# A decoder layer on one core: key products on VectorE in batches, rows turned for the expert gathers, and a new order of the attention steps

## The reference

```python
# sample: every token keeps 256 of 2049 keys, by indexer score, and attends to the gathered rows
_, idx = lax.top_k(sc, topk)
kg, vg = ck[phys, off], cv[phys, off]          # 256 rows of 512 floats per sample, keys and values
s = einsum('bthd,btkhd->bthk', q, kg) * 64**-0.5;  p = softmax(s);  out = einsum('bthk,btkhd->bthd', p, vg)
# prompt: 8 heads of sparse attention over <= 256 keys, mask from the indexer's top 64;
#         4 heads of attention into 256 memory tokens without a mask
m = g0 * (conv @ w_br_conv) + g1 * (attn @ w_br_attn) + g2 * (mem @ w_br_mem)
h = LN(ALPHA * x + m @ w_o)
# 32 experts (1024 -> 2*256 -> 1024), 2 per token inside the best of 4 groups
y = sum_e gate[:, e] * ((silu(h @ up_e[:, :256]) * (h @ up_e[:, 256:])) @ w_down[e])
out = LN(ALPHA * h + y)
```

## Time and profile before

| | |
|---|---|
| median of 3 runs | 612.38 us (610.49 to 614.92) |
| profiled execution, device time | 612.95 us |
| profiled execution, span of the records | 611.1 us, so 1.85 us lie around it |
| TensorE busy | 551.1 us (90%) |
| VectorE busy | 277.9 us (45%) |
| ScalarE busy | 101.1 us (17%) |
| GpSimd busy | 63.9 us (10%) |
| moved by DMA | 163.53 MB, 268 GB/s over the span |

### The profile page before, as it was taken

One profiled execution on the slowest core, in us unless ns is written; L12 is line 12 of the kernel. 1 busy time (PEld: TensorE's weight loads), 2 busy tenths in 40 slices (PEclk: granted clock), 3 DMA queues, 4 the chain that ended last, 5 costly groups with the idle time before them and its releaser, 6 DMA issues.

```text
span 611.1 us, 8674 instructions
## 1 busy us (share of the span) xinstructions
PE 551.1 (90%) x3518; PEld 348.4 (57%) x3518; DVE 277.9 (45%) x766; ACT 101.1 (17%) x243; POOL 63.9 (10%) x70
## 2 busy tenths in 40 slices
PE   7999999999999995999799899999999995987671
PEld 4556566475688773777576456766654661522120
DVE  1273765666677687759862496312010200100026
ACT  1001111011310123545100211011101110101011
POOL 0000000000200034587200000000000000000002
PEclk9999999998999996999899997999999999897796
DMA  8981231944443445576869926899999999999971
GB/s 294 372 321 45 93 138 50 365 140 140 131 132 120 139 138 189 175 242 190 330 247 403 321 70 262 306 417 388 424 390 422 420 419 420 422 419 421 417 302 71
DMA packets 47886, 163.53 MB, mean 268 GB/s; under 512 B 5954, under 2 KB 22812, under 8 KB 35812
## 3 DMA queue, kind: packets, MB, share of 16 engines
q1 hardware_dynamic: 39280, 139.81, 59.4%
q0 software_dynamic: 3472, 14.31, 6.9%
q10 hardware_dynamic: 5092, 8.83, 4.0%
HBM read 160.14 MB, written 2.77 MB: 267 GB/s over the span
## 4 chain that ended last, share of the span: by engine, by line
PE 57%; DMA 17%; DVE 17%; ACTq 5%; issue 2%; ACT 1%; SPq 0%; POOLq 0%; POOL 0%; DVEq 0%
PE bank L578 11%; DMA ring<-in_w_down 10%; PE bank L769 10%; PE bank L1122 6%; DMA ring<-in_w_up 5%; PE bank L539 4%; PE bank L1214 2%; PE bank L965 2%; ACTq L1476 2%; PE bank L624 2%; ACTq L1475 2%; DVE ring L1686 2%; PE bank L1079 2%; PE bank L1097 2%; PE bank L592 2%
## 5 line engine op out<-in xcount | busy, mean ns | idle before, releaser
L769 PE MATMUL bank<-work,ring 128*128 128x264 f32 x384 | 94.1, 396 | 0.0
L578 PE MATMUL bank<-ring,work 128*128 128x512 f32 (+2 forms) x224 | 90.6, 544 | 2.1 <-DMA ring<-in_w_in 2.1
L769 PEld LDWEIGHTS bank<-work,ring 128*128 128x128 f32 x384 | 71.2, 192 | 14.8 <-issue 2.8
L1122 PE MATMUL bank<-ring,work 128*32 128x512 f32 x304 | 52.4, 665 | 14.2 <-DMA ring<-in_w_up 11.0
L578 PEld LDWEIGHTS bank<-ring,work 128*128 128x128 f32 x224 | 40.0, 190 | 32.8 <-issue 29.7
L2350 DVE SCALAR_TENSOR_TENSOR work<-work,bank 128x256 f32<-128x256 f32 x8 | 3.4, 422 | 87.0 <-ACT work L1530 87.0
L2362 DVE COPY gates<-bank 128x512 f32<-128x512 f32 x8 | 5.5, 692 | 74.7 <-PE bank L1214 67.7
L895 PE MATMUL bank<-work,ring 128*128 128x264 f32 x128 | 32.6, 400 | 4.3 <-DVE gates L2091 4.3
L1122 PEld LDWEIGHTS bank<-ring,work 128*32 128x32 f32 x304 | 13.9, 121 | 37.5 <-issue 37.4
L1122 PE MATMUL bank<-proj,work 128*32 128x512 f32 x128 | 30.6, 622 | 2.3 <-DMA ring<-in_w_up 1.9
L895 PEld LDWEIGHTS bank<-work,ring 128*128 128x128 f32 x128 | 24.0, 195 | 12.5 <-DVE gates L2091 5.1
(11 more groups left out here) (337 smaller groups left out, 845.1 us busy)
## 6 DMA issues: line engine op xcount, KB each, us to landing
ring<-in_w_up SPq DMA_DIRECT2D x19, 2048.0 KB, 19.8
ring<-in_w_down SPq DMA_DIRECT2D x13, 2048.0 KB, 24.3
ring<-in_w_in SPq DMA_DIRECT2D x22, 1024.0 KB, 5.9
proj<-in_w_up SPq DMA_DIRECT2D x8, 2048.0 KB, 20.7
misc<-in_w_up SPq DMA_DIRECT2D x5, 1024.0 KB, 25.9
gates<-in_w_up SPq DMA_DIRECT2D x5, 1024.0 KB, 20.2
ring<-in_w_o SPq DMA_DIRECT2D x4, 1024.0 KB, 8.7
proj<-in_w_down SPq DMA_DIRECT2D x2, 2048.0 KB, 24.3
```

What stands on the lines that cost most here:

```text
L578: last = mm(bank[2 * (i % 2) + t][:, 0:w], lhs[:, k, 128 * t:128 * t + 128], rhs[:, k % 4, :], start=(k == 0), stop=(k == KT - 1))
L769: last = mm(b[:, 0:TOK], w[:, k, 128 * (n % 2):128 * (n % 2) + 128], xT[:, k, 0:TOK], start=(k == 0), stop=(k == KT - 1))
L1122: last = mm(bank[5][32 * j:32 * j + 32, :], xTe[q // 2 % 2][:, k, s0:s0 + CAP], up_of(n + j // 2, j % 2, r), start=(k == 0), stop=(k == KT ...
```

## The change

It has several parts, and none alters what is computed.

- **Keys.** GpSimd only issues DMAs: 16 key gathers without a wait between them, then 16 value gathers. VectorE multiplies all 17 key rows, in place and several rows to an instruction (groups 3, 4, 5, 2, 2 and 1 rows), and sums them likewise.
- **Memory heads.** `softmax(n)` for n < 4 no longer writes scaled scores: the maximum is taken from the score bank, two numbers are scaled, and `exps(n)` reads the bank with a scale of 0.125. `head_out(p)` moves to ScalarE.
- **Order in attention.** `scores(0)` moves ahead of `gate_tile(11)`, `softmax(0)`, `softmax(1)` and their inverses come earlier, no top-k round stands between index steps any more, `scores(p + 1)` stands between the two `turn`s of a pair, and three small VectorE steps move ahead of the compaction.
- **Order in the merge.** The last key products stand behind `merge(2)`; `sample_max` comes after `branch_tile(5)`, the later sample steps are put between other branch tiles.
- **Turned rows.** `h3` is stored turned, number k * 128 + q instead of q * 8 + k, so that a gather's weight operand is a run of 128 numbers. ScalarE copies tiles 0 and 2 from `ytmp` (`h_copied`), VectorE writes tile 1 (`ln_scale_turned`) and a second time untouched into `ytmp`. The ALPHA residual now reads `ytmp`: `residual_tile(0)` and `residual_samples` move in between parts of `wo_second`, `residual_tile(1)` behind `up_half(0, 1)`.
- **DMA.** The constant table waits for the first weight unit instead of `x`; a half of an expert's down weights (`down_0[1]`) is issued two positions later.

```diff
-KEY_PRODUCTS = ((), range(0, 3), range(3, 6), range(6, 9), range(9, 12), ())
-KEY_DOTS = ((), (), range(12, 13), range(13, 15), range(15, 17), ())
+KEY_SUMS = ((), ((0, 3),), ((3, 7),), ((7, 12),), ((12, 14),), ((14, 16), (16, 17)))
+        hturn = gate_t[:, 0:3072].rearrange("p (t k q) -> p t q k", t=3, k=KT)
...
@@ sync
                 if n == NU_WO:
-                    sp.wait_ge(kd_mul, NPROD)
-                    sp.wait_ge(kd_dot, NDOT)
+                    sp.wait_ge(kd_sum, NSUMS)
...
-                if p == NWS:
+                if p == NWS + 2:
                     sp.wait_ge(route_ready, 1)
                     sp.dma_start(down_0[1], e0[:, 1]).then_inc(aside_in, 16)
@@ tensor
             gate_tile(10)
             index_scores(0)
+            scores(0)
             gate_tile(11)
...
             index_scores(2)
-            scores(0)
             gate_tile(13, part=0)
...
                 turn(2 * p)
-                turn(2 * p + 1)
                 if p + 1 < PAIRS_H:
                     scores(p + 1)
-                ahead, behind = PAIR_TILES[p]
                 if p == 0:
                     gate_tile(14, part=1)
+                turn(2 * p + 1)
...
-                    sample_max(1, H)
                     branch_tile(4)
-                    branch_tile(5)
-                    sample_spread(1, H)
                 values(p)
...
+            branch_tile(5)
+            sample_max(1, H)
             branch_tile(6)
+            sample_spread(1, H)
             branch_tile(7)
+            branch_tile(8)
             sample_sum(1, H)
-            branch_tile(8)
             branch_tile(9)
...
-            wo_second(0, (0, 1, 2, 3, 4, 5, 7, 6)).then_inc(wo_ps, 1)
+            wo_second(0, (0, 1, 2, 3, 4))
+            pe.wait_ge(h_ready, 1)
+            pe.wait_ge(aid_ready, 1)
+            residual_tile(0).then_inc(res_ps, 1)
+            wo_second(0, (5, 7, 6)).then_inc(wo_ps, 1)
...
             wo_second(1, range(4))
+            pe.wait_ge(h_ready, 2)
+            residual_samples().then_inc(res_ps, 1)
...
-                        last = mm(bank[6 + b][:, 128 * kk:128 * kk + 128], h3[:, t, 4 * b + kk::KT], Ssl[:, t, 0:128],
+                        last = mm(bank[6 + b][:, 128 * kk:128 * kk + 128], h3[:, t, 128 * (4 * b + kk):128 * (4 * b + kk) + 128], Ssl[:, t, 0:128],
...
+            pe.wait_ge(h_ready, 3)
+            residual_tile(1)
             gate_turn(0)
@@ scalar
-            act.wait_ge(x2_in, 16)
-            act.dma_start(cst[:, 128:nconst], a["consts"][:, 128:nconst]).then_inc(cst_in, 16)
...
+            act.wait_ge(unit_sem(0), UC[0])
+            act.dma_start(cst[:, 128:nconst], a["consts"][:, 128:nconst]).then_inc(cst_in, 16)
...
+                    src, scale = (score_bank(n)[:, at:at + w], 0.125) if n < NMH else (s, 1.0)
+                    act.activation(s, src, ACT.Exp, bias=stats[:, st + t:st + t + 1], scale=scale,
...
+            def h_copied(n, t, m):
+                act.wait_ge(h_ready, n)
+                act.activation(hturn[0:m, t], ytmp[0:m, :].rearrange("p (q k) -> p q k", k=KT), ACT.Copy).then_inc(hp_ready, 1)
@@ gpsimd
-                pool.tensor_tensor(prod[i % 4], Kg[:, i, :], qrep, ALU.mult).then_inc(kd_mul, 1)
...
+            for i in range(16):
+                key_gather(i)
+            pool.wait_ge(sa_p, 4)
+            for i in range(16):
+                value_gather(i)
@@ vector
+            def key_sum(i0, i1):
+                if i0 == 0:
+                    dve.wait_ge(qr_sb, 1)
                     dve.wait_ge(knew_in, 32)
+                    dve.wait_ge(kg_in, 16 * 16)
+                n = i1 - i0
+                rows = Kg[:, i0:i1, :] if i0 < 16 else knew.unsqueeze(1)
+                tt(rows, rows, qrep.unsqueeze(1).broadcast_to([128, n, AW]), ALU.mult)
+                link(V.tensor_reduce(ssc[:, H * i0:H * i1].rearrange("p (i h) -> p i h", i=n),
+                                     rows.rearrange("p i (h d) -> p i h d", d=HD), AX.X, ALU.add), kd_sum)
...
+                if n < NMH:
+                    link(V.tensor_reduce(st[:, 0:2], score_bank(n)[:, :].rearrange("p (t n) -> p t n", t=2),
+                                         AX.X, ALU.max, negate=True))
+                    ts(st[:, 0:2], st[:, 0:2], 0.125, s=at_m)
+                    return
...
+            def ln_scale_turned(x, t, lnb, done_sem):
+                link(V.scalar_tensor_tensor(hturn[:, t], x.rearrange("p (q k) -> p q k", k=KT),
...
+            merge(2)
+            for i0, i1 in KEY_SUMS[PAIRS_H - 1]:
+                key_sum(i0, i1)
+            merge(3)
             sample_max(H, 17, sbias)
```

More of the change, by code:

```diff
@@ L978, in logits, with residual_tile, residual_samples @@
                 return last
+            def residual_tile(t):
+                for dh in range(2):
+                    last = mm(bank[2 * t + dh][:, :], alpha_id, ytmp[:, 512 * dh:512 * dh + 512], start=True, stop=False)
+                return last
+            def residual_samples():
+                for j in range(4):
+                    last = mm(bank[4][32 * j:32 * j + 32, 0:256], alpha_id[0:NS, 0:32],
+                              ytmp[0:NS, 256 * j:256 * j + 256], start=True, stop=False)
+                return last
             pe.wait_ge(r_ready, 1)
@@ L1035, in _ @@
             mm(bank[5][:, 64:96], ones[:, 0:128], mask[:, 0:32], start=False, stop=False)
-            mm(bank[5][:, 64:96], ones[:, 0:128], mask[:, 64:96], start=False, stop=True).then_inc(pos_ps, 1)
-            first_part(1, range(4), (0, 2))
+            mm(bank[5][:, 64:96], ones[:, 0:128], mask[:, 64:96], start=False, stop=True)
+            for t in range(3):
+                last = mm(bank[5][:, 96:128], ones[:, 0:128], mask[:, 32 * t:32 * t + 32], start=(t == 0), stop=(t == 2))
+            last.then_inc(pos_ps, 1)
+            pe.wait_ge(hp_ready, 3)
             pe.wait_ge(first_s, 2)
-            pe.wait_ge(h_ready, 3)
             for b in range(2):
                 first_part(b, range(4), (1,)).then_inc(first_ps, 1)
-            for t in range(3):
-                last = mm(bank[3][:, 0:32], ones[:, 0:128], mask[:, 32 * t:32 * t + 32], start=(t == 0), stop=(t == 2))
-            last.then_inc(cnt2_ps, 1)
+            pe.wait_ge(cnt_read, 1)
             def first_gather(i):
@@ L1464, in _ @@
                     normalise(2 * p + 3)
+                head_out(p)
                 if behind is not None:
@@ L2041, in _ @@
             tt(Alo, Alo, scan[:, 0:128].unsqueeze(2).broadcast_to([128, 128, 16]), ALU.mult, comp_in)
+            softmax(0)
             dve.wait_ge(comp_ps, 4)
@@ L2096, in _ @@
                 w = 128 * (t + 1)
-                for r in range(*INDEX_ROUNDS[i]):
-                    topk_round(r)
                 dve.wait_ge(is_act, i + 1)
@@ L2220, in _ @@
             dve.wait_ge(ht_ps, 2)
-            ln_scale(h3, 0, 1, lnb, ytmp, h_ready)
+            ln_scale(ytmp, 0, lnb, h_ready)
             dve.wait_ge(wo_ps, 2)
@@ L2310, in _ @@
             route(LATE, 1)
-            ln_scale(h3, 1, 3, lnb, ytmp, h_ready)
+            ln_scale_turned(ytmp, 1, lnb, hp_ready)
             dve.wait_ge(pos_ps, 2)
@@ L2314, in _ @@
             first_slots(0, LATE, 1)
+            link(V.tensor_reduce(rt[:, 143:144], bank[5][:, 96:128], AX.X, ALU.max), cnt_read)
+            ln_scale(ytmp, 1, lnb, h_ready)
             tt(eg, lgg, b3(m3, 4), ALU.subtract)
```

254 lines of the change are left out of this document (102 added, 152 removed).

## The result

The changed kernel took 632.31 us (median of 4 runs, 629.01 to 633.08) against 611.43 us before (4 runs): ratio 1.0337, 95% interval 1.0274 to 1.0399. It is slower by 3%, where 598 us was forecast. The profiled execution took 629.01 us, its records span 627.1.

What follows compares the result with a forecast made beforehand. TensorE sets the pace up to 370 us, then a DMA-bound expert weight stream starting at SyncE's issue at 370.83. Terms -1.0 - 10.1 - 2.7 + 1.0 - 2.3 = -15.1 us gave 598 us, range 594.5 to 601.5 (chance 0.60).

Steps and rivals of the forecast that it cites:

- Part 1: Kernel start: issuing the constant table later lets the first weights land sooner, -1.0 us (bounds 0 to -2.1).
- Part 2: Attention heads 0 to 3: the new order turns head 4 at 253.6 instead of 263.72, -10.1 us (-6 to -10.8).
- Rival 3: Key products wait for unlimited gathers in flight that slow each other to 4.4 us: 635 us, chance 0.04.
- Part 3: Head pairs and keys, key products on VectorE: head 8 to `sample_values` takes 21.7 us, -2.7 us (0 to -4.9).
- Part 4: From `sample_values` until the expert weight stream starts: TensorE gets the ALPHA residuals, +1.0 us (0.5 to 3).
- Part 5: First expert gathers: faster instructions on turned rows shrink holes in the weight stream, -2.3 us (0 to -4.0).
- The sum: Whole kernel: the five parts add to -15.1 us, 597.9 from the profiled 612.95, forecast as 598.
- the range of 592 to 606: Whole kernel: the measured time lies from 592 to 606 us with a chance of about 0.84.

Runs made afterwards that it cites:

- e17: The changed kernel as it is, run again on chip 0: 632.60 us, ratio 1.0298 to the kernel before.
- e18: The changed kernel with key gathers two in flight and value gathers four per pair of heads, on chip 0: 609.48 us, ratio 0.994.
- e3: The changed kernel with value gathers four per pair of heads and key gathers without a limit, on chip 5: 612.06 us, ratio 0.9981.
- e1: The changed kernel with key gathers two in flight and value gathers four per pair of heads, on chip 5: 608.22 us, ratio 0.993.
- e12: The changed kernel as it is, run again on chip 8: 599.64 us, ratio 0.9806 to the kernel before (2 runs).
- e13: The changed kernel as it is, run again on chip 15: 602.34 us, ratio 0.9833 to the kernel before.
- e15: The changed kernel as it is, run again on chip 7: 601.88 us, ratio 0.9847 to the kernel before.
- e2: The changed kernel with only the key gathers held to two in flight, value gathers back to back, on chip 5: 608.13 us, ratio 0.9924.
- e9: The changed kernel, gathers still without limit, but each list's completions on two semaphores in turn instead of one, on chip 8: 601.94 us.

## Why the prediction was wrong

Two things together cost the 31 us: gathers issued back to back from 218 us on, and something around the run that lets this hold up TensorE. The pair e17 and e18 shows the first (same chip, gathers held back, 23 us less); so does, on chip 5, the pair e3 and e1, which differ in the key gathers alone (e1 has two in flight and two semaphores for them), and of which only e3 has a stretch. The pairs e17 against e12, e13 and e15 show that the second exists (same kernel, 31 us apart), but not what it is: chip and time changed together from group to group. The forecast had a term for neither.

- **Part 1** (-1.0) was not had. The idle time before the first chunk did fall, from 2.10 to 1.05 us in the first measurement and 1.15 in e12, but only because the transposes ahead of it end later. The chunk itself starts at 10.33 and 10.22 instead of 10.44 (9.4 was forecast), and at 10.48 in e15: a gain of 0.2 us at most. The table's DMA is issued at 10.22 instead of 6.57 in the first measurement, and the first unit of weights hardly lands earlier for it. That e12 reaches gate tile 12 at 217.10, 1.5 us ahead of the kernel before, comes mostly from the granted clock between 148 and 157 us, the first row of these windows being the kernel before, the second e12, the third e15:

```profile
148.00:157.00 9.00, 8.69 (x30) 4.62 (x31) 2.77 (x12) 3.28 (x11) 0.00 (x0) 0.81 0.39 117
148.00:157.00 9.00, 8.74 (x39) 4.98 (x38) 3.87 (x14) 3.43 (x12) 0.00 (x0) 1.00 0.39 117
148.00:157.00 9.00, 8.65 (x31) 4.74 (x32) 2.90 (x13) 3.40 (x12) 0.00 (x0) 0.81 0.39 117
```

  e12 and e15 are the same kernel, so this is not the change's doing; e15 issues its first gather 1.8 us later than e12.
- **Part 2** (-10.1) is the step that failed: "So head 4 is turned at 253.6 instead of 263.72". It was turned at 282.81. The working behind it holds where TensorE is not held up: e12 has `softmax(4)` at 246.71 (248.4 forecast), and takes 34.4 us from gate tile 12 to head 4 (251.54 - 217.10) where 35.0 was forecast and 45.1 measured before, -10.7. What it left out is any cost of the burst of gathers for TensorE. It counted TensorE's own work and the waits of the program, and put what GpSimd and the DMA engines do beside it at nothing. That missing term measured 31.3 us (282.81 against 251.54).
- **Rival 3** named the right change, "Gathers in flight without a limit", and nearly the right time (635), but by a wrong mechanism, and so with a chance of 0.04. Its condition was a slow gather, over 3.3 us; the gathers were fast, some 42 us for all 32, and keys were never late. The argument against it, "at 170 GB/s the DMA engines are 0.56 busy", looked at bandwidth, and bandwidth was not what ran out: from 238 to 262 us e12 moved 298 GB/s, e17 254 and the first measurement 208. Its first half does bite with the old limit of two: e2 and e18 show VectorE waiting 7.7 and 8.1 us. The statement of part 3 that the values "are early for their users" is right in both measurements.
- **Part 3** (-2.7): -2.4, in the first measurement and in e12. Head 4 to head 8 took 19.62 us; a batch of three rows 1.76 and 1.75 us, of four 2.29 each, as priced. `branch_tile(5)` waited 1.77 us (1.3 forecast).
- **Part 4** (+1.0): +2.4 in e12 and +2.2 in the first measurement, inside its bounds. The traces of e13 and e15 take 68.8 and 67.0 us from `sample_values` to the issue, +5.7 and +3.9 against the 63.08 before, above the bound of 3; their granted clock is below 1.00 in places here (e13 0.76 in 293 to 300 and 0.86 in 350 to 362), where e12 has 1.00.
- **Part 5** (-2.3): -3.6, inside its bounds. The first 32 gather instructions, 7.86 us before, took 3.82 us in the first measurement, in e13 and in e15 (119 ns each, about 110 forecast) and 5.44 us in e12, where the granted clock was 0.69. The slot release came 17 us after the issue instead of 24.1. The turned write of tile 1 took 2.01 us where the straight one takes 1.28, so a write at that stride costs 0.73 us: the Trainium skill, page "SBUF — State Buffer", section "Door 1: The DMA port swizzle", by which each access to a new 16-byte line pays, points the right way, and paying in full as the weight read does (2.6 us) is too much.
- **The sum**: in e12 -12.2 + 0 - 2.4 + 2.4 - 3.6 + 0.6 (tail) = -15.2 us against -15.1 forecast, 597.81 us profiled against 597.9. So close a match is in part luck: of the -12.2 some -10.7 is part 2, -0.2 part 1 and -1.3 the rest ahead of gate tile 12, mostly that clock, and parts 4 and 5 are off by 1.4 and 1.3 us in opposite directions. On the three chips without the stretch the medians, 599.64 to 602.34, lie in the range of 592 to 606; the two measurements with it do not.

What stays open: what differs between the groups (the chip, the time, where the program and its tensors lie in memory, what else the chip does), and by which path the gathers hold up TensorE. The rows show late instructions and late signals together, not what blocks them. Nor is a rule of issue rate shown: in e2 the value gathers follow one another with few gaps from 256 us on, on a chip where e3 had a stretch, and nothing is late. And every run that escaped the stretch on chips 5 and 0 had its key completions on two semaphores, every one that had it on one; against that, the 16 value gathers of e2 follow closely on one semaphore. Theory F, that the one semaphore does it, was tested only on chip 8 (e9), where the unchanged kernel had no stretch either. The limit of four, the best kernel that also bounds its queue (599.48 and 601.67 us), was not run on a chip with the stretch; on chips without it, it is no faster than the changed kernel. The version that beat both there is e18, by 0.6% against the kernel before and 3.7% against the changed one (609.48 / 632.60).

## What to carry to other kernels

A limit on outstanding gathers that looks like a plain wait can be what keeps the other engines at their pace; when it is taken out, ask what the burst costs each engine that works beside it, not only the users of the data. Read "issue" gaps at multiples of a fixed time inside a group without waits, and "remote" waits for work that is long done, as an engine held up from outside the program, not as missing data. Before a late packet is called the cause, count how far its engine had come. Read the gain of a shorter wait from the start of what stood behind it, not from the idle time. And run the unchanged kernel beside its variants from the first experiment on: seven variants were read against a stretch that their chips may not have had.

## What the runs showed of the hardware

- One program, one input, two times: 599.64, 602.34 and 601.88 us on chips 8, 15 and 7, 632.60 us on chip 0, each within 1% over its own runs, while the kernel before differed by 0.4% over all six chips. Each chip was used at one time only.
- During the stretch TensorE starts its instructions at multiples of 0.70 us, 22 of them in the 19.7 us from 238.39 to 258.08; its signals reach ScalarE and VectorE 18 to 28 us late, while a signal from ScalarE still reaches VectorE within 0.1 us (ReLU until 232.27, sum from 232.37). The granted clock falls with it, to a mean of 0.61 in 238 to 262 us and 0.50 in 245 to 258, which is the lower of its two levels (1.2 and 2.4 GHz), and the first gate tile after it takes 5.83 instead of 3.83 us.
- Packets on the queues of kind "instruction" come at fixed places of the program, not at fixed times: after 95 and 96 matmuls from 221 us on, at 266 to 269 us in the first measurement and at 236 to 239 in e12.
- Two executions of one kernel (e12 and e15) differ in the granted clock of 148 to 157 us, 1.00 and 0.81, and four matmul instructions of 512 columns there take 1.98 and 3.12 us.
- The Trainium skill, page "SBUF — State Buffer", section "SBUF: two separate sides", says that a DMA and a compute operation cannot slow each other, their ports being apart. Against e18, e17 shows TensorE slowed while gathers run all the same; in the first measurement instructions and signals are late and no row shows a wait for a port, so the sentence on the ports may hold and yet not be enough to plan by.
